# A slot table moved: the sample tile's routing heads 11 slots apart from slot 944, its attention steps four slots apart

## The reference, cut to what matters

```
q_sb, k_sb, v_sb, q_sw, k_sw, v_sw = split(rms_norm(x) @ w_in)
o_sb = stick_breaking(q_sb, concat(cache_sb_k, k_sb), concat(cache_sb_v, v_sb))   # sample; the prompt has no cache
o_sw = sink_window_attention(q_sw, k_sw, v_sw)                                    # window of 128 tokens
h = x + concat(rms_norm(o_sb), rms_norm(o_sw)) @ w_out
q = rms_norm(h) @ w_q                              # 8 heads, two halves of 128
i1, i2 = top16(q[:, 0] @ keys_1.T), top16(q[:, 1] @ keys_2.T)
idx, gate = top16 of the 256 sums, softmax         # 16 of 16384 experts for each token and head
y = h + sum_k gate_k * gelu(u[idx_k] . x) * v[idx_k]
return rms_norm(y), and the new keys and values
```

## Time and profile before

| | us |
|---|---|
| median of 3 runs | 3407.89 (3405.43 to 3410.37) |
| the profiled execution | 3406.38 |
| its span | 3404.2 |
| granted TensorE clock, mean | 0.877 |

### The profile page before, as it was taken

One profiled execution on the slowest core, in us unless ns is written; L12 is line 12 of the kernel. 1 busy time (PEld: TensorE's weight loads), 2 busy tenths in 40 slices (PEclk: granted clock), 3 DMA queues, 4 the chain that ended last, 5 costly groups with the idle time before them and its releaser, 6 DMA issues.

```text
span 3404.2 us, 38082 instructions
## 1 busy us (share of the span) xinstructions
PE 2575.5 (76%) x10640; PEld 1207.4 (35%) x10640; DVE 2221.5 (65%) x5631; ACT 1385.1 (41%) x3204; POOL 1627.8 (48%) x1634
## 2 busy tenths in 40 slices
PE   7989887678668767877787768877877777777665
PEld 6845332343224322432243224432343233322321
DVE  2024665587667866776677766776677667775775
ACT  2021353454336423653365335543565354542222
POOL 0101445544555555545554554555454645455553
PEclk9989898888879888989898878988999889878777
DMA  5544999998999999999999999999999999999887
GB/s 182 173 134 158 350 364 413 370 364 332 399 390 385 380 411 389 384 368 405 381 396 362 388 392 356 387 381 410 364 389 377 409 387 405 386 390 380 354 354 296
DMA packets 271315, 1216.27 MB, mean 357 GB/s; under 512 B 29808, under 2 KB 122272, under 8 KB 134912
## 3 DMA queue, kind: packets, MB, share of 16 engines
q0 software_dynamic: 154560, 1113.51, 82.4%
q1 hardware_dynamic: 116544, 100.33, 9.2%
HBM read 1193.05 MB, written 20.79 MB: 357 GB/s over the span
## 4 chain that ended last, share of the span: by engine, by line
PE 36%; DMA 22%; DVE 12%; issue 8%; ACT 6%; POOL 6%; DVEq 2%; ACTq 2%; SPq 0%; POOLq 0%
DMA f_uv<-peer_uv,f_idx 19%; PE f_y_acc L1527 17%; PE f_q_ps L1466 6%; DVE f_uv L1041 5%; POOL f_uv L826 4%; PE f_z L1315 3%; PE f_z L1430 2%; PE f_y_acc L1409 2%; ACT f_diag L970 2%; ACT L964 2%; POOL f_gate_fold L814 2%; PE f_z L1296 2%; PE f_z L1322 1%; DMA f_work<-cache_sb_kT 1%; ACTq L968 1%
## 5 line engine op out<-in xcount | busy, mean ns | idle before, releaser
L826 POOL DMA_INDIRECT f_uv<-peer_uv,f_idx x1056 | 1288.5, 1220 | 1586.6 <-PE f_y_acc L1527 1292.2
L1041 DVE CUSTOM_DVE_ANT_0 f_uv<-f_uv,f_x_rep 128x1024 f32<-128x1024 f32 x1056 | 1301.8, 1236 | 746.8 <-DMA f_uv<-peer_uv,f_idx 741.4
L1527 PE MATMUL f_y_acc<-f_uv,f_diag 128*64 128x512 f32 x4224 | 1264.3, 721 | 603.3 <-ACT f_diag L970 568.1
L1527 PEld LDWEIGHTS f_y_acc<-f_uv,f_diag 128*64 128x64 f32 x4224 | 302.2, 155 | 1234.0 <-ACT f_diag L970 739.3
L964 ACT ACTIVATE f_act_hid<-f_hid 128x2 f32<-128x2 f32 x528 | 107.2, 203 | 1284.5 <-DVE f_hid L1041 1282.6
L1466 PE MATMUL f_q_ps<-r_w_q,f_xnT 128*128 128x256 f32 x1152 | 316.2, 427 | 76.5 <-DVE f_cut L1167 76.5
L970 ACT ACTIVATE f_diag<-f_gate_fold,f_act_hid 128x64 f32<-128x64 f32 x1056 | 310.0, 340 | 38.6 <-issue 1.7
L814 POOL TENSOR_TENSOR f_gate_fold<-r_fold,f_gates 128x128 f32<-128x128 f32 x528 | 311.7, 590 | 9.5
L1466 PEld LDWEIGHTS f_q_ps<-r_w_q,f_xnT 128*128 128x128 f32 x1152 | 236.6, 214 | 186.6 <-DVE f_cut L1167 93.5
L964 ACT ACT_TABLE_LOAD x195 | 250.2, 1283 | 3.4
L839 ACT ACT_TABLE_LOAD x119 | 152.7, 1283 | 219.3 <-PE f_z L1296 177.4
(11 more groups left out here) (174 smaller groups left out, 2589.8 us busy)
## 6 DMA issues: line engine op xcount, KB each, us to landing
f_uv<-peer_uv,f_idx POOLq DMA_INDIRECT x1056
f_work<-scratch_projT SPq DMA_DIRECT2D x86, 128.0 KB
w_cols<-w_in SPq DMA_DIRECT2D x18, 512.0 KB, 4.0
r_w_out<-w_in SPq DMA_DIRECT2D x18, 512.0 KB, 4.3
f_work<-out_sb_v_prompt SPq DMA_DIRECT2D x72, 128.0 KB
r_w_q<-w_peer_q SPq DMA_DIRECT2D x8, 1024.0 KB, 7.2
x_in<-x_prompt SPq DMA_DIRECT2D x8, 512.0 KB, 5.2
f_q_pad<-scratch_projT SPq DMA_DIRECT2D x64, 64.0 KB
```

Of the source, the lines that this page charges most:

```text
L826: pool.indirect_dma_start(uv[:, n % RING, :], None, io["peer_uv"], bass.IndirectOffsetOnAxis(ap=idx[:, t % 2, head, k:k + 1], axis=0),).th ...
L1041: nc.vector.tensor_tensor_reduce(row_u, row_u, x_rep[:, g % 2, :], 1.0, 0.0, ALU.mult, ALU.add, hid[:, n // 2 % 8, n % 2:n % 2 + 1]).then_ ...
L1527: last = nc.tensor.matmul(y_acc[i * GT:(i + 1) * GT, b * 512:(b + 1) * 512], diag[:, batch % 3, i, :], uv[:, n % RING, DM + b * 512:DM + ( ...
```

## The change

Two expressions in the slot table, both for t = NT alone:

```diff
@@ def route_slot(t, head):
-    return t * P - 77 + 15 * head if t < NT else t * P - 63 + 9 * head
+    return t * P - 77 + 15 * head if t < NT else t * P - 80 + 11 * head
@@ def step_slot(t, e):
-    return window_slot(t, 0) - 6 - (4 if t < NT else 5) * (steps_of(t) - e)
+    return window_slot(t, 0) - 6 - 4 * (steps_of(t) - e)
```

## The result

The change made the kernel slower. Nine runs of the changed kernel have a median of 3428.23 us (3414.45 to 3515.73), nine of the one before 3404.14; the ratio is 1.0081, interval 1.0057 to 1.0106. Beside the experiments, four more runs gave 1.0067 (1.0048 to 1.0087). So it is 0.7 to 0.8%, 23 to 28 us, where 11 were forecast.

What follows compares the result with a forecast made beforehand. The prediction took the DMA engines to bound the kernel, so their idle time sets the cost. Its terms, -18 + 27 + 2 = +11 us, took the profiled 3406.38 to 3417, with 1.5 for the median 3419; range 3387 to 3434.

Steps and rivals of the forecast that it cites:

- What bounds the kernel: Whole kernel: the DMA engines set the pace, bytes stay the same, so only their idle time (holes) changes the time.
- Part 1: Sample's heads, 11 slots apart instead of nine: queries' wait for `cut` and seven DMA holes go, about -18 us.
- the eighth hole: DMA idle time at the sample's last head, 2.2 us, with no queries behind it; forecast to stay.
- Part 2: Sample's steps, four slots apart instead of five: key load no longer fits, long and short steps alternate, +27 us.
- Part 3: Windows and tail 17 slots earlier, meeting other stages' DVE work: +2 us, bounds -1.6 and +5.
- The covered load: Rival at the steps: gathers already issued cover the key load's wait; sum about -18 us, 3390; chance 0.26.
- DVE's lag: Rival at the heads: DVE's 2.5 us lag, not the wait for `cut`, makes the holes; 3434 us; chance 0.09.
- The draw: Rival: key loads cost some 18 us instead of 27, so nothing measurable is left; 3408 us; chance 0.15.

## Why the prediction was right or wrong

**What bounds the kernel**: right in the main. No byte of the two queues changed, and most of each move is a move of DMA idle time: 24 of 31 us at the heads, 51 of 63 in the steps. The other 12 us of the steps are no holes. The stretch moved 315 x 302.1 us = 95.2 MB against 393 x 239.3 us = 94.0, some 3 us, and the queues ran at 315/0.83 = 380 GB/s while busy, where before had 393. Why they were slower was not tested.

**Part 1, the heads (-18)**: the mechanism is shown, the size was too small. Queries one slot later, with DVE untouched, gave -24 us; ten apart gave -20; in the change the heads' stretch fell by 31. Two steps of the sum were mis-sized. I left 0.5 us of hole at each of seven heads and the eighth hole whole; after shows a share of 1.00, so nothing was left of the 220 x 0.11 = 24 us of idle time which the stretch had. The other 7 us are not holes. From the two rows, 354 x 220 us are 77.9 MB and 406 x 188 us 76.3, so some 4 us are bytes that fell outside the stretch; the rest is the rate, 354/0.89 = 398 GB/s while busy before, 406 now. Neither was foreseen, and with profiles that differ by a few us here the second is barely more than their spread.

**Part 2, the steps (+27)**: the load's part of the mechanism is shown, the size was half or less. The load no longer fits (17.8 us in four slots), long and short steps alternate, and the waits stand at seven of 16 steps. Alone it costs 51 us. My price for V ahead of K was 3.1 us at each of eight long loads, 24 us; undoing the order gave 17 and 4 us a wait. The rule of the Trainium skill ("DMA: Bandwidth & Descriptors", Queues, rings and completion order), that a ring's descriptors are consumed in order, agrees with that run. The turns of pieces with rows of gathers are in the trace of after. From 2853 to 2860, inside a long load, the two queues passed the same number of pieces (packets, MB, share):

```profile
q0 software_dynamic: 371, 2.70, 92.8%
q1 hardware_dynamic: 371, 0.19, 9.2%
```

And the 2 KB layout agrees: the same bytes in a quarter of the pieces, 18 us down to 9 to 11.

The term that was mis-sized is the hole behind a wait. I took 9 us of wait, let the gathers already issued cover 4, and got 3.8 for each. The waits were shorter, 6.7 us in the mean: the block came a little later than forecast (17.7 to 19.2 us for 17.1), but PE stood ready 9 to 13 us after the issue, not 7.6. The holes were longer, 48/7 = 6.8. The gathers already issued did cover the waits: over the seven of them the DMA share was 0.91 to 1.03. The hole stands almost wholly behind the wait. The cover of 4 was read off two waits of before, and held the way of before from a wait's end to the next gather; the forecast had no term for a longer way. In the step above, first the wait itself and then the time behind it (us, POOL busy, PEclk, DMA share, GB/s):

```profile
2855.07:2862.10 7.03, 0.34 (x1) 0.68 1.03 415
2862.10:2866.00 3.90, 0.00 (x0) 0.50 0.42 172
```

A buffer comes free only when `scores`, `values` and a pair of experts are done (2862.10 to 2868.7), and POOL issues at 2869.48, 7.4 us after the wait's end. Over the seven waits this was 7.0 to 10.4 us; over the six waits above 1 us in before, 3.7 to 6.3. There the experts followed `scores` directly, as behind the wait of 4.47 us of rows 10; PE and then POOL:

```profile
2746.90 3.38 PE L1527 MATMUL f_y_acc<-f_uv,f_diag 128*64 128x512 f32 x8
...
2751.06 0.95 POOL L826 DMA_INDIRECT f_uv<-peer_uv,f_idx  x1 [7.73 <-PE f_y_acc L1527]
```

In the change `values` stands between, 1.92 us. The clock adds to this time in both kernels: at the end of the wait the granted clock is 0.50 (1.2 GHz), and `scores` took 1.94 us, `values` 1.92 and the pair 2.89, where the next ones at full clock took 1.00, 1.08 and 1.94. So POOL stood still for 14.1 to 20.8 us in the changed kernel, and for up to 9.9 in before. That the move of `values` makes the difference is read from this order and was not tested by an edit. The forecast of a share near 0.87 and 220 us was too mild: 0.82 and 263.

**Part 3, windows and tail (+2)**: between 2 and 5 us by dots 902 to 970 against the kernel before and against the run with steps alone, which is within the spread of single profiles. But I looked for the price among DVE's stages, and a part of it lies with SP: the last value block is issued behind the windows' loads, and its wait of 6.6 us in after (14.6 with steps alone and short key loads) belongs to the steps' new place. This wait was missed altogether.

**The sum.** 3419 was forecast and 3428 measured, and that they lie so near is partly luck. By dots Part 2 was 36 us too low and Part 1 13 us too small a gain, and the two errors work against each other. The forecast also stood on a median of three runs, 3407.89, where nine gave 3404.14. As a difference, 11 us were forecast and 23 to 28 measured.

**The rivals.** The covered load falls: its condition was waits under some 5 us, they came to 6.7 us in the mean, and 48 us of holes stood behind them. DVE's lag falls. The draw is excluded by the interval, and the kernel that comes nearest to it is the one with K ahead of V.

## What to carry to other kernels

In a kernel that lives on one queue of large gathers, count what a change does to the time in which that queue is empty, and never let the work that frees its buffers stand behind a long wait of another stage. Price such a wait from its start to the next gather, with all the work between its end and the first buffer that comes free. A load that competes with large rows lasted here by its number of pieces: 512 pieces of 512 bytes took 18 us, 128 of 2 KB 9 to 11. When a hand-made table is tightened, look at every single-buffered load: its reach in slots is its deadline, and two loads that used to be released in different slots may come to stand one behind the other.

## What the runs showed that was not expected

The unchanged part of the program, from the first dot to dot 820, took between 2356.8 and 2383.5 us in the twelve profiled executions, a spread of 27 us that follows no edit. One profile against one profile would have shown half of the change's effect; the stretch of changed dots, and several runs, were needed.

After a wait of 7 us the DMA engines were idle in two pieces, not in one (shares of 0.04 from 2864 to 2866 and 0.02 from 2869 to 2871), and the loads issued in between passed at 0.59; the key block landed in 3.2 us, where the one before had taken 17.7. A slow load makes the next one fast: half of the steps pay, and a mean over all loads would hide it.

A move of four slots for five changed the number of activation table loads, 40 to 72 in one stretch, without a line of the program saying so. A slot table sets the order on ACT too, and the order decides how often its tables are swapped.
